# First output projection over eight PSUM banks, the key load moved into it, and three low halves given to VectorE

## The reference

```
x = x + (g_m * a_m + g_f * a_f + g_c * a_c) @ p['w_out']
x = x + peer_ffn(rmsnorm(x, p['norm_ffn']), p['peer_wq'], p['peer_keys'], p['peer_u'], p['peer_v'])
```

```
def peer_block(tok, wq, keys, u, v):
    p = tok.shape[0]
    qr = (tok @ wq).reshape(p, PEER_HEADS, 2, PEER_DQ // 2).astype(jnp.float32)
    s = jnp.einsum('phcd,hckd->phck', qr, keys.astype(jnp.float32))
    top_s, top_i = lax.top_k(s, PEER_TOPK)
...
```

## Time and profile before

| what | value |
| --- | --- |
| median of 3 runs | 1929.91 us (1926.39 to 1932.4) |
| profiled execution | 1931.49 us |
| its span on the core | 1929.8 us |
| TensorE busy | 1827.1 us (95%) |
| VectorE busy | 1566.1 us (81%) |
| GpSimd busy | 1068.1 us (55%) |
| ScalarE busy | 860.4 us (45%) |

### The profile page before, as it was taken

How to read it: one execution, slowest core, us unless ns; L and a number is a source line. 1 busy time by engine, 2 the same in 40 slices (tenths; PEclk the granted TensorE clock), 3 DMA queues, 4 the chain that set the end, 5 groups by cost and what they waited for, 6 DMA issues and landing times.

```text
span 1929.8 us, 34458 instructions
## 1 busy us (share of the span) xinstructions
PE 1827.1 (95%) x12531; PEld 1206.1 (62%) x12542; DVE 1566.1 (81%) x2939; ACT 860.4 (45%) x1310; POOL 1068.1 (55%) x671
## 2 busy tenths in 40 slices
PE   9999999999998989999978999998999999999996
PEld 7647777777777756566545666664555555555554
DVE  7975566455357589999979999995699999999997
ACT  6444446565445534333435666662333333333331
POOL 2732122222245748667688888888455555555551
PEclk9999999999999989999999999999999999999998
DMA  5732114223354545678799999999999999999993
GB/s 204 217 106 91 55 56 122 97 76 107 134 171 156 183 151 166 211 239 289 269 387 343 405 414 416 415 378 405 377 399 401 401 402 402 393 400 396 400 363 131
DMA packets 178077, 517.61 MB, mean 268 GB/s; under 512 B 19032, under 2 KB 61024, under 8 KB 177448
## 3 DMA queue, kind: packets, MB, share of 16 engines
q1 hardware_dynamic: 85280, 246.22, 35.3%
q0 software_dynamic: 55296, 201.35, 27.2%
q10 hardware_dynamic: 37384, 68.50, 9.8%
HBM read 458.55 MB, written 57.46 MB: 267 GB/s over the span
## 4 chain that ended last, share of the span: by engine, by line
PE 39%; DVE 26%; DMA 23%; issue 4%; POOL 4%; ACT 3%; ACTq 1%; SPq 0%; DVEq 0%; POOLq 0%
DMA raw<-in_v_units 21%; PE ps L1942 17%; PE ps L2061 10%; DVE rows L1699 4%; PE ps L1958 3%; DVE w_lo L1828 2%; POOL w_lo L601 2%; ACT w_hi L725 2%; DMA rows<-in_u_rows,rowi 2%; PE ps L2215 2%; POOL rows L627 1%; DVE accS L1848 1%; DVE hot L1808 1%; DVE hot_hi L1811 1%; PE ps L2195 1%
## 5 line engine op out<-in xcount | busy, mean ns | idle before, releaser
L601 POOL TENSOR_TENSOR w_lo<-raw,w_hi 128x1024 bf16<-128x1024 f32 x253 | 554.7, 2200 | 489.6 <-ACT w_hi L725 450.7
L725 ACT ACTIVATE w_hi<-raw 128x1024 bf16<-128x1024 f32 x381 | 400.2, 1053 | 452.1 <-DMA raw<-in_v_units 274.5
L660 POOL DMA_INDIRECT rows<-in_v_units,rowi x192 | 290.9, 1515 | 238.3 <-DVE accS L1848 190.0
L1942 PE MATMUL ps<-h_hi,w_hi 128*128 128x384 bf16 x1024 | 337.8, 330 | 17.7 <-ACT hb L1119 17.7
L2444 PE MATMUL ps<-W_hi,w_hi 128*128 128x384 bf16 x992 | 324.9, 327 | 21.4 <-DVE W_lo L1866 19.6
L1942 PE MATMUL ps<-h_lo,w_hi 128*128 128x384 bf16 x1024 | 337.6, 330 | 0.0
L1942 PE MATMUL ps<-h_hi,w_lo 128*128 128x384 bf16 x1024 | 337.3, 329 | 0.0
L2444 PE MATMUL ps<-W_hi,w_lo 128*128 128x384 bf16 x992 | 324.3, 327 | 0.0
L2444 PE MATMUL ps<-W_lo,w_hi 128*128 128x384 bf16 x992 | 324.2, 327 | 0.0
L1699 DVE CUSTOM_DVE_ANT_0 rows<-rows,ps 128x1024 f32<-128x1024 f32 x192 | 227.5, 1214 | 39.6 <-DMA rows<-in_u_rows,rowi 38.4
L627 POOL DMA_INDIRECT rows<-in_u_rows,rowi x192 | 201.7, 1051 | 98.0 <-DVE dots L1699 52.9
(11 more groups left out here) (469 smaller groups left out, 3415.1 us busy)
## 6 DMA issues: line engine op xcount, KB each, us to landing
raw<-in_u_units SPq DMA_DIRECT2D x128, 512.0 KB, 5.5
raw<-in_v_units SPq DMA_DIRECT2D x128, 512.0 KB, 12.3
raw<-in_units SPq DMA_DIRECT2D x123, 512.0 KB, 3.2
hd<-hb ACTq DMA_DIRECT2D x128, 192.0 KB, 6.2
Hb<-hd SPq DMA_DIRECT2D x32, 768.0 KB, 11.2
gd<-gsb ACTq DMA_DIRECT2D x48, 384.0 KB, 9.4
Gb<-gd SPq DMA_DIRECT2D x32, 576.0 KB, 8.4
gz<-stage ACTq DMA_DIRECT2D x24, 288.0 KB, 2.1
```

Source lines behind the costliest of these rows:

```text
L601: pool.tensor_tensor(w_lo[:, k % RING, :], raw[:, k % RAW, :], w_hi[:, k % RING, :], ALU.subtract).then_inc(lo_ready, 1)
L660: pool.indirect_dma_start(out=rows[:, (ND + n) % RG, :], out_offset=None, in_=table, in_offset=bass.IndirectOffsetOnAxis(ap=index, axis=0))\
L725: act.activation(w_hi[:, k % RING, :], raw[:, k % RAW, :], ACT.Copy).then_inc(hi_ready, 1)
L1942: last = pe.matmul(ps[:, bank + half, 0:n], w[:, slot, col:col + P], x(k)[:, half * n:(half + 1) * n], start=(k == 0 and w is w_hi and x i ...
```

## The change

Group A's output projection writes tile j to bank j, so TensorE waits for no addition within it. Query tile 0, which writes bank 2, now waits for all eight additions, and so does tile 1. The load of the keys is issued by ScalarE behind the high half of unit 86 and not behind the last block. The low halves of units 87, 89 and 91 (`LOW_A`) are made by VectorE, behind its work at tiles 5, 6 and 7; GpSimd leaves them out and waits, ahead of the unit behind each, until it is done. GpSimd's loop of eight units ends at unit 79 and not at 95; the units from there are written out.

```diff
+LOW_A = {5: U_WQ + 2, 6: U_WQ + 4, 7: U_WQ + 6}
@@ gpsimd
-            with pool.Fori(1, U_OUT2 // RING) as i:
+            with pool.Fori(1, U_WQ // RING) as i:
                 for k in range(RING):
                     low_half(i * RING + k, k)
-            for n in range(U_OUT2 // RING * RING, U_PEER + RING):
+            for n in range(U_WQ // RING * RING, U_PEER + RING):
+                if n in LOW_A.values():
+                    continue
+                if n - 1 in LOW_A.values():
+                    pool.wait_ge(lo_ready, n)
                 low_half(n, n)
@@ scalar
             for j in range(KT):
                 high_unit(U_OUT + j + RING)
+                if j == 1:
+                    act.dma_start(keys[:, :, :], a["keysT"]).then_inc(keys_in, 16)
                 if j:
                     out_high_a(j - 1)
             out_high_a(KT - 1)
-            act.dma_start(keys[:, :, :], a["keysT"]).then_inc(keys_in, 16)
             root(2, rA[:, 0, :], ps[:, 0, 0:2])
@@ vector
+            def low_a(n):
+                dve.wait_ge(hi_ready, n + 1)
+                dve.wait_ge(lo_ready, n)
+                dve.tensor_tensor(w_lo[:, n % RING, :], raw[:, n % RAW, :], w_hi[:, n % RING, :],
+                                  ALU.subtract).then_inc(lo_ready, 1)
             for j in range(KT):
                 dve.wait_ge(unit_used, U_OUT + j + 1)
-                dve.tensor_tensor(xT[:, j, TD:T], ps[:, j % 2, 0:NA], xT[:, j, TD:T], ALU.add).then_inc(x2_ready, 1)
+                dve.tensor_tensor(xT[:, j, TD:T], ps[:, j, 0:NA], xT[:, j, TD:T], ALU.add).then_inc(x2_ready, 1)
                 if j:
                     out_low_a(j - 1)
                 if j >= 2:
                     add_square(2, j - 1, sqA)
+                if j in LOW_A:
+                    low_a(LOW_A[j])
@@ tensor
             for j in range(KT):
                 n = U_OUT + j
                 pe.wait_ge(lo_ready, n + 1)
-                if j >= 2:
-                    pe.wait_ge(x2_ready, j - 1)
-                tile(n % RING, lambda k: mg_hi[:, k, mA], lambda k: mg_lo[:, k, mA], j % 2, n=NA, halves=1,
+                tile(n % RING, lambda k: mg_hi[:, k, mA], lambda k: mg_lo[:, k, mA], j, n=NA, halves=1,
                      ready=None if j else 0, split=g_mlo).then_inc(unit_used, 1)
@@
             for q in range(NHC):
                 n = U_WQ + q
                 pe.wait_ge(lo_ready, n + 1)
-                if q >= 2:
-                    pe.wait_ge(q_evac, q - 1)
+                pe.wait_ge(*((q_evac, q - 1) if q >= 2 else (x2_ready, KT)))
```

## The result

The changed kernel takes 1935.05 us in the median of 20 runs (1931.77 to 1942.09), the kernel before 1929.64 (20 runs). The ratio is 1.0028, interval 1.0020 to 1.0036: 5.4 us slower (3.9 to 7.0 by the interval), a small loss, but clear of no change. The profiled execution has a span of 1935.1 us (1936.97 in all), 5.3 more than in the earlier trace rows.

A forecast was written before the change was run, and what follows sets the result against it. The prediction took VectorE's chain, held by GpSimd's low halves, to bound the stretch up to query tile 1. Late load and holds, +4.1 us on 1929.8, gave 1933.9, taken as 1934 us; range 1926 to 1939.

The forecast's parts named there:

- "same": Whole kernel: time within about 0.3%, or 5.8 us, of the kernel before; chance 0.80.
- the forecast's own case: Output projection into query tile 1: late load and holds add +0.5 to +5.2 us, 1930 to 1935 us; chance 0.65.
- step 2: Output projection: load of 91 issued at 608.2, landing at 611.4; ScalarE waits, so xg_hi 5 starts at 612.4, before 610.55.
- steps 4 and 5: GpSimd holds xg_lo 6 until 617.0 and the last addition until 620.8; query tile 0 +2.2 us, tile 1 +4.1 us.
- VectorE's back-to-back run: At 618.3, VectorE might keep the SBUF lock against GpSimd, leaving the last addition unheld; the sum would be +2.2 us.
- The sum: Start of query tile 1: 621.5 instead of 617.4, +4.1 us, passing through to the kernel's end.
- Eight banks: Output projection: stalls of 2.17 and 0.33 us removed, tiles end 2.5 us earlier, but VectorE's chain sets the end.
- the step that calls the loss of query tile 0's early start free: Query tile 0 waits for all eight additions; this costs nothing while the last xg_lo is later still.
- Value 0 both ways: Early keys load in the output projection: no gain or cost; without cover, a raw load late by up to 2.5 us.
- the slower rival: Query tiles: the clock comes back late after TensorE's idle time, 1.6 us per further tile, 1937 to 1940 us; chance 0.15.
- The rival of an early load: Output projection: unit 91 lands early, no raw wait on the path; -0.4 to -2.5 us, 1927 to 1930 us; chance 0.2.

The follow-up runs named there:

- e2_low: The kernel before with only the three low halves moved to VectorE, banks and keys as before; ratio 1.0029 to the kernel before.
- e3_actfirst: The changed kernel with ScalarE making xg_hi and the square of block j - 1 ahead of the high half of unit 85 + j; ratio 1.0002.
- e6_low_early: The changed kernel with VectorE's low halves of units 87 and 89 behind tiles 3 and 5, not 5 and 6; ratio 0.9986 to the kernel before.
- e10_again: The changed kernel once more, the same program, for a second trace and interval; ratio 1.0034 to the kernel before.
- e11_early_swap: e6_low_early with ScalarE making block j - 1 ahead of the high half of unit 85 + j; ratio 0.9974 to the kernel before.
- e1_banks: The kernel before with the eight banks alone, query tiles 0 and 1 waiting for all eight additions; ratio 0.9998.
- e9_hold2: The changed kernel with ScalarE's blocks first, all low halves on GpSimd, which waits before unit 87, and high halves from 91 made in the query stage; 0.9973 against before.
- e4_dummy: The kernel before with three unused subtractions added on VectorE at tiles 5, 6 and 7, GpSimd still making all low halves; ratio 1.0024.

## Why the prediction was right

The forecast of 1934 us and "same" was right in the mechanism and 1 us short; 1935.05 us lies at the upper end of the 1930 to 1935 us that the forecast's own case spans.

- *The load of 91* (step 2). Forecast: issued at 608.2, high half at 611.4, `xg_hi` 5 at 612.4. Measured 607.27, 610.55 and 611.51; the output tiles ran 1.9 us earlier than I had assumed, because the clock stayed at its high level there in this execution (1.00 where before has 0.57, worth 1.65 us). e2_low, e3_actfirst and e6_low_early show that this is the cause in the changed kernel.
- *The holds* (steps 4 and 5). Both came: 2.03 us on `xg_lo` 6, 2.27 us on the last `sqA`. VectorE's back-to-back run did not keep GpSimd out, which would have given +2.2 us; nor did it in e10_again, e2_low and e3_actfirst. In e6_low_early and e11_early_swap it did, with the operations in the same order and 0.15 to 0.16 us apart as here. What decides between the two, no run shows. The end of the last `sqA` was forecast at 620.8 and is 617.88 + 2.27 = 620.15.
- *The sum.* +4.1 us forecast to the start of query tile 1; measured +3.6 and +4.8 us there, and in all runs +5.4 (3.9 to 7.0 by the interval). But before's trace has the fall of the clock and the changed kernel's traces do not; at equal clocks the sum was 1 to 2 us short, by the estimate. That the raw trace difference comes so near to +4.1 is in part luck.
- *Eight banks.* In e1_banks the output tiles end 2.8 us earlier (the two stalls make 2.5; the forecast's own 611.5 less 608.7 is 2.8), and this was worth nothing, as forecast. In the changed kernel nearly the same came without the banks, as e2_low shows. And the step that calls the loss of query tile 0's early start free holds only behind the late `xg_lo`: alone it costs 1.8 us in the trace of e1_banks, though not in its runs.
- *Keys.* "Value 0 both ways" was wrong by a small term. The load of unit 89, beside the keys, kept ScalarE waiting until 602.30, 5.8 us after its issue at 596.45 where others take 3.2. In e10_again unit 90 was late as well: its load was issued at 596.50 and its high half starts 6.4 us later, behind 1.31 us of idle.

```profile
602.86 1.06 ACT L730 ACTIVATE w_hi<-raw 128x1024 bf16<-128x1024 f32 x1 [1.31 <-PE ps L1957]
```

  The profile names TensorE for this idle, but the tile in question had ended some 2 us before, so the load is what is left. These waits were not hidden: `xg_hi` 4 stands behind them in ScalarE's program, and the low half of 87 behind `xg_hi` 4. Counted from the first output matmul, the low half of 87 starts at 16.7 us in e2_low, where the keys come late, at 17.4 in the changed kernel and at 18.4 in e10_again, and the token sums at 31.2, 31.7 and 32.8. So the early keys cost about 0.5 and 1.6 us in the two traces; the runs cannot tell e2_low (1.0029) from the change (1.0028 and 1.0034). e6_low_early waits 1.3 and 0.9 us ahead of units 89 and 90, e11_early_swap 1.6 us ahead of unit 90.
- *The clock.* The low level ended within query tile 1 (1.00 from 625 us on), as before; the slower rival did not come.
- *The rival of an early load* put -0.4 to -2.5 us on a version in which nobody waits for 91. e6_low_early did -3.9 us in the stretch, or -2.2 at equal clocks, and -2.7 in the runs, which is at the rival's far end. I had left two holds in, and there is one (an `xg_lo` of 2.23 us at 606.45); and I had not counted that query tile 1 would then run at the high clock.

## What to carry to other kernels

When a step of a ring moves to a later place or another engine, follow the slot that it frees, and ask which engine stands in program order at the refill, and what is queued behind it: here a subtraction put off by 5 us cost nothing itself, but the load behind it did. Where two engines hold each other up, making one of them wait at the right time (e9_hold2, 0.9973) gives as much as moving work from one to the other at the right time (e11_early_swap, 0.9974). An early transfer is only free if the small ones that it runs beside have time to spare. And before a difference of a few microseconds between two traces is put down to a change, the granted clock in both is to be compared: here it hid 1.65 us.

## What I had not expected of the hardware

Adding three subtractions of 1.22 us to VectorE beside an unrelieved GpSimd cost 5.6 us of its time (3.15 for the first, e4_dummy). The hold goes both ways: in e6_low_early GpSimd's low half took 3.65 us and not 2.13 beside VectorE's short operations and its cast, while in the changed kernel the same order of starts held VectorE's `sqA` for 2.27 us. And a 512 KB load issued 1.5 us behind a 1 MB load was used only 5.8 us after its issue, where others come in 3.2.
